# A chunked gated delta rule on one core: one chunk after another, or three neighbouring chunks at a time

## What is computed

```python
# S_t = exp(g_t) S_{t-1} (I - beta_t k_t k_t^T) + beta_t k_t v_t^T ; o_t = S_t^T q_t
decay = exp(where(incl, g_cum[..., :, None] - g_cum[..., None, :], -inf))
a_mat = where(strict, beta[..., :, None] * (k @ k.T) * decay, 0.0) + eye(CHUNK)
rhs = concatenate([v * beta[..., None], k * (beta * exp(g_cum))[..., None]], axis=-1)
u, w = split(triangular_solve(a_mat, rhs, lower=True, unit_diagonal=True))
qk = where(incl, (q @ k.T) * decay, 0.0)
def step(state, xs):                                   # one chunk after the other
    v_new = u_c - w_c @ state
    o_c = qd_c @ state + qk_c @ v_new
    state = state * last_c + kd_c.T @ v_new
```

## Time and profile before

| | us |
|---|---|
| median of 3 runs (lowest, highest) | 4440.09 (4439.41, 4443.5) |
| profiled execution, its own time | 4443.01 |
| its span | 4441.0 |
| busy in the span: PE / DVE / ACT / POOL | 3583.1 / 2140.6 / 1107.1 / 1159.3 |
| granted TensorE clock, mean | 0.896 |

### The profile page before, as it was taken

How to read it: one execution, slowest core, us unless ns; L and a number is a source line. 1 busy time by engine, 2 the same in 40 slices (tenths; PEclk the granted TensorE clock), 3 DMA queues, 4 the chain that set the end, 5 groups by cost and what they waited for, 6 DMA issues and landing times. The chain is left out here.

```text
span 4441.0 us, 49671 instructions
## 1 busy us (share of the span) xinstructions
PE 3583.1 (81%) x18450; PEld 2762.6 (62%) x18450; DVE 2140.6 (48%) x3709; ACT 1107.1 (25%) x1965; POOL 1159.3 (26%) x654
## 2 busy tenths in 40 slices
PE   6787677657767677779999996689989778997978
PEld 4356555446666566568888785466756567665657
DVE  3579388774444424335555556503335450333552
ACT  2344133321112111110000001213335320333540
POOL 2013122212222344345444341231110233211112
PEclk7779889868888789889999998799989989998999
DMA  2001000000001111112221220210000121100011
GB/s 96 24 19 38 15 3 3 1 7 1 0 0 66 38 48 33 37 49 93 83 80 66 90 90 10 77 39 23 17 13 3 67 72 44 29 20 7 9 58 62
DMA packets 227900, 169.74 MB, mean 38 GB/s; under 512 B 42232, under 2 KB 214976, under 8 KB 226976
## 3 DMA queue, kind: packets, MB, share of 16 engines
q1 hardware_dynamic: 225152, 166.83, 12.0%
q10 hardware_dynamic: 2592, 0.81, 0.1%
HBM read 150.69 MB, written 16.92 MB: 38 GB/s over the span
## 5 line engine op out<-in xcount | busy, mean ns | idle before, releaser
L1434 DVE TENSOR_TENSOR I-12785S<-I-12785S,c_causal 128x256 f32<-128x256 f32 x64 | 27.7, 432 | 462.9 <-PE I-12785S L1372 462.9
L747 DVE TENSOR_TENSOR I-9738act_f<-I-9737act_g,I-9744p_u 128x1024 f32<-128x1024 f32 x22 | 26.9, 1222 | 321.9 <-PE I-9744p_u L259 167.3
L864 DVE SCALAR_TENSOR_TENSOR y_T<-y_T 128x1024 f32<-128x1024 f32 x48 | 131.9, 2786 | 0.0
L737 ACT ACTIVATE I-9737act_g<-I-9743p_g 128x1024 f32<-128x1024 f32 x22 | 22.6, 1029 | 419.5 <-PE I-9743p_g L259 419.5
L255 PE MATMUL I-9743p_g<-hf_hi,I-9719w_hi 128*128 128x512 f32 x352 | 109.5, 392 | 5.2 <-POOL hf_lo L473 5.2
L763 DVE TENSOR_TENSOR x_T<-x_T,I-9746p_d 128x512 f32<-128x512 f32 x176 | 112.5, 678 | 0.7 <-PE I-9746p_d L728 0.6
L763 DVE TENSOR_TENSOR x_T<-x_T,I-9745p_d 128x512 f32<-128x512 f32 x176 | 112.4, 677 | 0.4 <-PE I-9745p_d L728 0.4
L257 PE MATMUL I-9743p_g<-hf_lo,I-9719w_hi 128*128 128x512 f32 x352 | 109.0, 391 | 0.0
L259 PE MATMUL I-9743p_g<-hf_hi,I-9721w_lo 128*128 128x512 f32 x352 | 108.8, 390 | 0.0
L255 PE MATMUL I-9744p_u<-hf_hi,I-9720w_hi 128*128 128x512 f32 x352 | 108.4, 389 | 0.0
L257 PE MATMUL I-9744p_u<-hf_lo,I-9720w_hi 128*128 128x512 f32 x352 | 108.4, 389 | 0.0
(11 more groups left out here) (1035 smaller groups left out, 10457.1 us busy)
## 6 DMA issues: line engine op xcount, KB each, us to landing
y_T<-in_w_ada SPq DMA_DIRECT2D x48, 512.0 KB, 6.8
saved_x<-x_T SPq DMA_DIRECT2D x3, 4096.0 KB, 13.7
x_T<-saved_x SPq DMA_DIRECT2D x3, 4096.0 KB, 15.6
I-9717w_raw<-in_w_gate SPq DMA_DIRECT2D x22, 512.0 KB, 3.8
I-9718w_raw<-in_w_up SPq DMA_DIRECT2D x22, 512.0 KB, 4.1
I-12773w_raw<-in_w_in SPq DMA_DIRECT2D x16, 512.0 KB, 3.9
I-12774w_raw<-in_w_in SPq DMA_DIRECT2D x14, 512.0 KB, 3.9
I-9731d_raw<-in_w_down SPq DMA_DIRECT2D x11, 512.0 KB, 4.8
```

What stands on the lines that cost most here:

```text
L747: nc.vector.tensor_tensor(act_f[:, :], act_g[:, :], flat(p_u), ALU.mult).then_inc(product, 1)
L864: self.nc.vector.scalar_tensor_tensor(out=self.raw[s], in0=self.raw[s], scalar=1.0, in1=self.c_row, op0=ALU.mult, op1=ALU.mult, accum_out= ...
L1434: self.nc.vector.tensor_tensor(diag, diag, tiled(self.mask, 2), ALU.add).then_inc(self.masked, 1)
```

## The change

Only `delta_stage` is changed (some 220 lines become 430). The eight chunks are written out with Python constants; no hardware loop is left. Each part of a chunk becomes a small function of the chunk number, which does nothing outside 0 to 7, and each engine calls the pieces of chunk c+1's preparation and of chunk c-1's state move between the levels of chunk c:

```diff
-                for c in peeled(pe, NT):
-                    wait(pe, state_done, H * c)
-                    wait(pe, o_out, c)
...
+                for c in range(-1, NT + 1):
+                    below(c, 1)
+                    sum_gates(c + 1)
+                    double(c, 1)
+                    solve_values(c - 1)
+                    below(c, 2)
+                    solve_keys(c - 1)
+                    double(c, 2)
+                    key_products(c + 1)
+                    below(c, 3)
+                    take_state(c - 1)
+                    double(c, 3)
+                    turn_weighted(c + 1)
+                    ask_state(c - 1)
+                    below(c, 4)
+                    ask_chunk(c - 1)
+                    double(c, 4)
+                    turn_matrix(c + 1)
+                    add_keys(c - 1)
+                    below(c, 5)
+                    query_products(c + 1)
+                    double(c, 5)
+                    turn_keys(c + 1)
+                    below(c, 6)
+                    turn_values(c + 1)
+                    double(c, 6)
```

`below` is the product that makes Y, `double` the two that follow it. The other engines:

```diff
+# ACT, chunk c of range(-1, NT + 1)
+                    copy_below(c, 1)
+                    exponentials(c + 1)
+                    copy_below(c, 2)
+                    copy_keys(c - 1)
+                    copy_below(c, 3)
+                    copy_values(c - 1)
+                    copy_below(c, 4)
+                    copy_out(c - 1)
+                    copy_matrix(c + 1)
...
+# DVE, the same range
+                    subtract(c, 4)
+                    first_inverse(c + 1)
+                    move_state(c - 1)
+                    weigh_queries(c + 1)
+                    subtract(c, 5)
+                    scale_keys(c + 1)
+                    scale_values(c + 1)
+                    subtract(c, 6)
...
+# POOL, chunk c of range(-1, NT)
+                    for level in range(3, LEVELS):
+                        off_diagonal(c, level)
+                    spread_gates(c + 2)
+                    decay_queries(c + 1)
+                    off_diagonal(c + 1, 1)
+                    first_transposed(c + 1)
+                    off_diagonal(c + 1, 2)
```

The arithmetic changes in these places:

```diff
-                            v.tensor_tensor(T[:, heads, :], T[:, heads, :], g_T[g][:, heads, :], ALU.subtract).then_inc(doubled[g], 1)
-                            v.tensor_tensor(N[:, heads, :], N[:, heads, :], g_N[g][:, heads, :], ALU.subtract).then_inc(doubled[g], 1)
+                        v.tensor_tensor(TN[n % 2][g][:, :, :, :], TN[n % 2][g][:, :, :, :], p_TN[g][:, :, :, :], ALU.subtract).then_inc(doubled[g], 1)
...
-                    v.tensor_tensor(m_T[:, :, :], m_T[:, :, :], tiled(strict_t[:, :], H), ALU.mult).then_inc(weighted, 1)
...
-                    each(lambda h: mm(p_x[:, h, :], w_T[:, h, :], state[:, h, :], start=True, stop=True)).then_inc(ws_done, 1)
+                        last = mm(F[0][:, h, :], w_T[:, h, :], state[:, h, :], start=False, stop=(h == H - 1))
```

More of the change, by code:

```diff
@@ L2238, in delta_stage @@
     H = DN_HEADS
+    STEPS = LEVELS - 1
     GROUPS = [slice(0, H // 2), slice(H // 2, H)]
+    LAST = NT - 1
     with stage(nc) as st:
         big = lambda n: st.sb(n, [P, H, P])
[L2242 to L2245, removed]
@@ L2262, in delta_stage @@
[L2262 to L2267, removed]
+        both = lambda n: [big(f"{n}{s}") for s in range(2)]
+        TN = [[st.sb(f"TN{s}{g}", [P, 2, H // 2, P]) for g in range(2)] for s in range(2)]
@@ new lines, in delta_stage @@
+        q_dec, qk_T, v_beta, k_beta, k_dec = both("q_dec"), both("qk_T"), both("v_beta"), both("k_beta"), both("k_dec")
+        g_upper, d_T, e_cum, m_T, a_mat, a_T, Y, w_T, v_new, state = (big(n) for n in (
+            "g_upper", "d_T", "e_cum", "m_T", "a_mat", "a_T", "Y", "w_T", "v_new", "state"))
+        c_T = [big(f"c_T{level}") for level in range(1, LEVELS)]
+        neg_cum, rem, e_col, e_last, e_rem, kb_scale = (st.sb(n, [P, NT, H]) for n in ("neg_cum", "rem", "e_col", "e_last", "e_rem", "kb_scale"))
@@ L2269, in delta_stage @@
+        chunk = lambda t, h, n: t[:, h, n * P:(n + 1) * P]
+        heads = range(H)
+        inside = lambda n: 0 <= n < NT
+        t_of = lambda n, h: TN[n % 2][h // 2][:, 0, h % 2, :]
+        n_of = lambda n, h: TN[n % 2][h // 2][:, 1, h % 2, :]
+        halves = lambda t, g: t[:, GROUPS[g], :]
         with nc.Block() as block:
@@ L2277, in _ @@
             def _(pool):
-                nc.gpsimd.memset(state[:, :, :], 0.0).then_inc(state_set, 1)
[L2279 to L2311, removed]
+                def spread_gates(n):
+                    if not inside(n):
+                        return
+                    wait(pool, cum_done, n)
+                    nc.gpsimd.tensor_tensor(g_upper[:, :, :], tiled(upper[:, :], H), bcast(decay[:, n, :], P), ALU.mult).then_inc(spread, 1)
@@ new lines, in _, with sum_gates, key_products @@
+                mm, turn = nc.tensor.matmul, nc.tensor.transpose
+                def sum_gates(n):
+                    if not inside(n):
+                        return
+                    pe.wait_ge(spread, n + 1)
+                    wait(pe, a_copied, n)
+                    mm(F[2][:, :, :].rearrange("p h n -> p (h n)"), ones, g_upper[:, :, :].rearrange("p h n -> p (h n)"), start=True, stop=True).then_inc(cum_done, 1)
+                def key_products(n):
+                    if not inside(n):
+                        return
+                    wait(pe, qk_weighted, n)
+                    for h in heads:
+                        last = mm(F[3][:, h, :], chunk(k_T, h, n), chunk(k_T, h, n), start=True, stop=True)
+                    last.then_inc(kk_done, 1)
@@ new lines, in query_products, with turn_keys @@
+                def query_products(n):
+                    if not inside(n):
+                        return
+                    pe.wait_ge(weighted, n + 1)
+                    for h in heads:
+                        last = mm(F[3][:, h, :], chunk(k_T, h, n), chunk(q_T, h, n), start=True, stop=True)
+                    last.then_inc(qk_done, 1)
+                def turn_keys(n):
+                    if not inside(n):
+                        return
+                    wait(pe, o_out, n - 1)
+                    for h in heads:
+                        last = turn(F[1][:, h, :], chunk(k_T, h, n), ident)
+                    last.then_inc(k_turned, 1)
@@ new lines, in turn_values, with solve_values @@
+                def turn_values(n):
+                    if not inside(n):
+                        return
+                    wait(pe, state_done, H * (n - 1))
+                    for h in heads:
+                        last = turn(F[0][:, h, :], chunk(v_T, h, n), ident)
+                    last.then_inc(v_turned, 1)
+                def solve_values(n):
+                    if not inside(n):
+                        return
+                    for g in range(2):
+                        pe.wait_ge(doubled[g], STEPS * (n + 1))
+                    pe.wait_ge(v_scaled, min(n + 2, NT))
+                    for h in heads:
+                        mm(F[0][:, h, :], n_of(n, h), v_beta[n % 2][:, h, :], start=(h == 0), stop=False)
@@ new lines, in ask_state, with ask_chunk @@
+                def ask_state(n):
+                    if not inside(n):
+                        return
+                    pe.wait_ge(q_decayed, n + 1)
+                    for h in heads:
+                        last = mm(F[1][:, h, :], state[:, h, :], q_dec[n % 2][:, h, :], start=(h == 0), stop=False)
+                    last.then_inc(q_used, 1)
+                def ask_chunk(n):
+                    if not inside(n):
+                        return
+                    pe.wait_ge(v_ready, n + 1)
+                    pe.wait_ge(qk_weighted, n + 1)
+                    for h in heads:
+                        last = mm(F[1][:, h, :], v_new[:, h, :], qk_T[n % 2][:, h, :], start=False, stop=(h == H - 1))
+                    last.then_inc(o_done, 1)
@@ new lines, in add_keys, with below @@
+                def add_keys(n):
+                    if not inside(n):
+                        return
+                    pe.wait_ge(v_ready, n + 1)
+                    for h in heads:
+                        last = mm(F[0][:, h, :], k_dec[n % 2][:, h, :], v_new[:, h, :], start=True, stop=True)
+                    last.then_inc(kv_done, 1)
+                def below(n, level):
+                    if not inside(n):
+                        return
+                    pe.wait_ge(c_ready, STEPS * n + level)
+                    if level == 1:
+                        pe.wait_ge(t_set, n + 1)
+                        pe.wait_ge(n_set, 2 * (n + 1))
+                    for g in range(2):
+                        if level > 1:
+                            pe.wait_ge(doubled[g], STEPS * n + level - 1)
+                        for h in heads[GROUPS[g]]:
+                            last = mm(p_Y[g][:, h, :], c_T[level - 1][:, h, :], t_of(n, h), start=True, stop=True)
```

(26 more changed lines are left out.)

316 lines of the change are left out of this document (185 added, 131 removed).

## The result

The changed kernel takes 4289.48 us (median of 4 runs, 4287.45 to 4290.97) against 4441.8 (4439.41 to 4451.33) in the same comparison: a ratio of 0.9653, 95% interval 0.9636 to 0.967. The prediction was 4294, range 4278 to 4320.

The account below looks back on a forecast made before the run. Before, chains from engine to engine bound each chunk; after, PE's 26.1 us plus 1.5 waiting. 990.0 + 24.6 + 165.6 + 23.0 + 9.6 = 1212.8 against 1358.4: 145.6 us shorter, 4294 on the median's scale, range 4278 to 4320.

Parts of the forecast that it names:

- stage start to the first Y: Ahead of chunk 0's doubling: first sum at 976.4, 9.0 to a_T, 4.6 for c_T and N; doubling starts at 990.0.
- chunk 0's body: Chunk 0's doubling, 21.3, with chunk 1's preparation inserted: +0.5 each for sum and query product, +2.3 at DVE's crowded place: 24.6 us.
- six bodies of 27.6: The full middle bodies, PE's work plus 1.5 us of waiting each, 165.6 us together.
- chunk 7's levels and its own move: Last chunk: levels with only chunk 6's state move inserted, 23.0 us, then its own move with the wait, 9.6.
- PE's work in a body: Matmul groups, transposes and gate sum of a middle chunk: 26.1 us if PE never waits.
- Rival 2: Levels stay chains and inserted pieces add: bodies of 30.0 us, 18 us more, 4313; chance 0.17.
- The pause ahead of level 6: PE waits for DVE's level 5 subtraction, 1.4 us and 0.1 for the second group, making the body 27.6 us.
- POOL's half: POOL's half-size instruction between DVE's third and fourth of the first inverse: taken as 0.65 us, bounds 0.42 and 1.26.
- Rival 1: No turns: POOL and DVE don't meet, body 26.1, chunk 0 loses its 2.3, 11 us less, 4283; chance 0.14.
- Turns with POOL: In the first inverse DVE and POOL exclude each other on SBUF: DVE's third and fourth instructions 0.8 to 1.7 us, first two 0.42.
- Rival 4: Clock never rises: short waits keep PE at 1.2 GHz, 52.2 us of work a chunk, slower, 4490; chance 0.03.
- Rival 3: Code arrives late: written-out stage needs fetches, two a chunk at 3.8 us for seven chunks, 53 us, 4347; chance 0.07.

## Why the prediction was right

The mechanism held: PE's own work sets a body, and one pause is left, at the forecast place. The whole sum was 8.6 us short, with all four terms off the same way. From memset to the last state move's end the stage went from 389.95 to 235.74 us, 154.2 less, where the sum had 145.6. That the kernel's time is only 4.5 us off 4294 is in part luck: the medians moved by 152.3, 6.7 more than the sum, but the median before was 1.7 higher in this comparison, and 0.5 went in rounding.

| step of the prediction | forecast | measured | off |
|---|---|---|---|
| stage start to the first Y (21.5 = 990.0 − 968.5) | 21.5 | 19.95 | −1.6 |
| chunk 0's body | 24.6 | 22.6 | −2.0 |
| six bodies of 27.6 | 165.6 | 161.2 | −4.4 |
| chunk 7's levels and its own move | 32.6 | 32.0 | −0.6 |

- **PE's work in a body**, 26.1: right to 0.1. Bodies without a pause are 26.0, and 0.89 us more of work made them 0.90 longer. Rival 2 (the pieces add, 30.0) falls with that.
- **The pause ahead of level 6**: right in place, cause and the two stretched instructions, too long in size, 1.5 forecast and 0.86 measured (26.86 − 26.00). The step that was mis-sized is the sum over DVE's queue there. I had added durations; starts in a full queue are closer. The state move takes 1.12 but the next starts 1.03 after it, the 0.68 of the queries 0.60, and the first inverse took 2.96 from its start to the state move's, not 3.4. POOL's half, which had no row and was put at 0.65, took 0.91 beside DVE and 0.73 alone. Its bound was counted too high in the prediction: the layout has one such half ahead of DVE's fourth instruction, so 1.26 would have added 0.6 us to a body, not 1.2. Rival 1 (no turns) falls: about its 26.1 is what one gets by making POOL wait.
- **Turns with POOL**: 1.49 and 0.94 us with POOL reading, 0.42 and 0.42 with POOL held back, and 1.50 where another product of POOL was met. The other cause that the prediction named, two engines on one tile, falls, since none of these pairs shares one. The Trainium skill ("SBUF — State Buffer", "Who interferes with whom") has the rule that a DVE instruction with two SBUF inputs contends with a GpSimd instruction that reads SBUF. The trace agrees.
- **The clock**: 1.00 in every full body, 0.96 over the stage for 0.87. Rival 4 falls.
- **Chunk 0's body**, 24.6 against 22.6: the forecast took 21.3 for its six levels from the kernel before, 1.3 above six of 3.34, because the first ran at the lower clock there. In this execution it ran at the higher one. With the first inverse or the state move put elsewhere on DVE it ran at the lower one again, and the body took 25.0 and 25.6, so the sign of this term is chance.
- **Late code**: bodies 26.86 apart to 0.01, and their one wait, of 0.7 us, has a known releaser. Rival 3 falls. The page of the profile shows 112 and 61 instruction packets for 100 and 56, so more code was brought, but beside the work.
- **The start**: the columns took 2.15 (975.21 to 977.36), not 2.8, and sum to first Y 12.8, not 13.6.
- **What hadn't been asked**: how much of the gain is overlap. The prediction compared timelines and needn't know; my first guess in the experiments, 25 us without overlap, was far off. By stage length, in one trace each: 45.4 us come with the rewritten chain, 25.7 with the next sum no longer waiting for the state (the clock that goes with it included), 82.7 with the pieces among the levels. By the ratios of whole kernels it is about 38, 19 and 97. What in the rewritten chain brings its share stays open.

## What to carry to other kernels

When chains through several engines leave the main engine idle, add up that engine's own work in the interleaved body, then lay out the other engines' queues against it. The time is the work plus what is late in the most crowded queue, and the latter is better added up from start to start than from durations, where the instructions follow each other without waiting (1.03 for 1.12 and 0.60 for 0.68 here). A piece moved out of a crowded place frees it only if nobody waits for that piece: the state move, put later, gave PE a new wait. And before a gain is put down to overlap, run the same pieces in serial order; here between a third and a half of it was still there.

## What the runs showed of the hardware

Chunk 0's first level ran at either clock, in kernels that are alike up to there. In the changed kernel its first Y's two groups start 0.52 apart, and the granted clock is 1.00 from 990.12 on. With the first inverse moved they start 0.99 apart, and it is 0.50 (1.2 GHz) for the 6.1 us from 998.39 to 1004.50:

```profile
990.12 0.68 PE L2449 MATMUL I-5723p_Y<-I-5679TN,I-5703c_T 128*128 128x128 f32 x4 [1.45 <-POOL I-5680TN L2304]
990.64 0.61 PE L2449 MATMUL I-5724p_Y<-I-5680TN,I-5703c_T 128*128 128x128 f32 x4
```

```profile
998.39 1.19 PE L2449 MATMUL I-5723p_Y<-I-5679TN,I-5703c_T 128*128 128x128 f32 x4 [1.44 <-POOL I-5680TN L2304]
999.38 1.06 PE L2449 MATMUL I-5724p_Y<-I-5680TN,I-5703c_T 128*128 128x128 f32 x4
```

Both came after the same work and the same 1.45 us without matmuls. Even one and the same kernel had both: with POOL held back chunk 0's body took 22.05 us in one execution and 23.49 in the other, where its first level ran partly at the lower level. With all pieces among the levels chunk 0's body was 22.1 to 25.6 us long, for the most part by this. The start of the stage also moved, from 964.5 to 980.0 us into the span in profiles of kernels with the same code ahead of it; what does that wasn't looked into, and it is one reason to look for a change of 5 us in the stage's own length.
